# Weighting and turning the gathered expert rows by products with diagonal matrices on the tensor engine

## The chip, the cores and the metric

One Trainium2 chip, one core. The metric is the device time of one execution of the whole program in microseconds (us), median of several runs. TensorE is called PE below, VectorE DVE, ScalarE ACT, GpSimd POOL, SyncE SP. "PEclk" or "granted clock" is TensorE's clock as a share of 2.4 GHz: 1.00 is 2.4 GHz and 0.50 is 1.2 GHz.

## What is computed

Two layers of a hybrid backbone over 256 latent and 256 context tokens of width 1024. Each layer first mixes tokens (attention, a long convolution, a short convolution) and then runs a mixture of 16 experts, of which two work for each token. The end of a layer is the part that matters here: for each token the rows of its two experts are weighted, added, multiplied by a per-channel gate and added to x. The next layer starts with a root-mean-square norm of that x and a modulation by shift and scale.

```python
wts = jnp.take_along_axis(s, eidx, axis=1)
wts = wts / jnp.sum(wts, axis=-1, keepdims=True)
...
y = (jax.nn.silu(t @ w_gate[e]) * (t @ w_up[e])) @ w_down[e]
out = out + combine[:, e:e + 1] * y
...
x = x + gt2 * y[:, :s]
xc = xc + cgt2 * y[:, s:]
...
y = xf * lax.rsqrt(jnp.mean(xf * xf, axis=-1, keepdims=True) + NORM_EPS)
```

## The kernel before

The program is written engine by engine: each engine has its own list of instructions, run in the order of the code, and semaphores tie them together. Nothing reorders them. x lives in SBUF as `xT`, channels on partitions (8 tiles `k` of 128) and 512 tokens along the free axis. The experts' outputs are written as token rows to a tensor in DRAM, `y_rows`.

The passage of this case lies between the two layers (`l` = 0 at its end, called the passage below). It is walked once, for four groups `t` of 128 tokens:

- ACT issues the last four DMAs of expert outputs into `y_rows` (line 1240). DVE waits until all of them have landed (lines 2136 and 2137, semaphore `y_out`) and sets `rows_ok`.
- POOL waits for `rows_ok`, then issues eight indirect DMAs (line 833), two for each `t`, which gather the rows of the token's first and second expert into `yg[:, t, 0, :]` and `yg[:, t, 1, :]`, 512 KB each.
- ACT scales the first row by its weight into `comb` (`scale_first`, lines 1344 to 1349), DVE multiplies the second by its weight and adds it (line 2148), PE turns the sum with eight transposes (line 2846, shown in the trace under the helper's line 2181), and DVE multiplies the result by the gate and adds it to `xT` in eight steps (line 2156).
- For the next layer's norm ACT squares the new `xT` (`next_square`, lines 1351 to 1355), PE sums the squares over channels with a matrix of ones (`next_sums`, line 2833, eight products for each `t`), DVE scales the sums (line 2165), ACT takes the root (line 1375) and DVE the reciprocal (line 2168). The two halves of the tokens (latent, context) have one root each. Then DVE clears the semaphores (line 2171), and that sets `layer_done`, for which all engines wait.

Beside it the next layer's weights are prepared. SP issues eight loads of 1 MB of modulation weights, the leads 0 to 7 (in the trace `lead<-in_mod`, and `spare<-in_mod` for leads 6 and 7), then two loads of 1 MB of input weights (`stage<-in_in`, `unit(l + 1, ...)`), and a third of modulation weights (`stage<-in_mod`) once PE has used lead 6 (lines 738 to 750). PE multiplies the leads by the conditioning vector (`lead_units`, line 2223 in the trace) after its last expert work; leads 4 to 7 share one wait, for all four. The two input weights are split into a high part by ACT (`whi`, line 1361) and a rest by DVE (`wlo`, lines 2141 to 2143, in the trace under line 1391). `modulation` (line 1439) is a group of three small DVE steps on the result of the leads.

## Time and profile before

| what | value |
|---|---|
| median of 3 runs | 1332.89 us (1331.44 to 1336.42) |
| profiled execution | 1330.76 us |
| its span | 1328.9 us |
| mean granted clock of TensorE | 0.959 |
| PE busy | 1215.8 us, 91% |
| DVE busy | 661.7 us, 50% |
| ACT busy | 412.9 us, 31% |
| POOL busy | 128.4 us, 10% |
| passage, from the landing of the last expert rows to the clearing of semaphores | 777.6 to 812.0 us |

The span is the time between the first and the last recorded instruction; the profiled execution's own time is 1.9 us longer. The shares are averages over the whole program; what is changed lies in one stretch of 34 us, and that stretch has to be read by itself, in the chain of waits and in the engines' timelines. In a timeline row a group of like instructions is merged: start, time to the end of the last, engine, line, what, count, and in brackets the idle time before them and what ended it.

### The profile page before, as it was taken

Reading aid. Unit: us, or ns where it says so; the run is one execution under the profiler, and the core shown is the slowest. Engines: PE = TensorE matmul, PEld = TensorE weight load, DVE = VectorE, ACT = ScalarE, POOL = GpSimd, SP = SyncE. Lnnn points to the kernel's source line nnn. Section 1 sums busy time; section 2 is a strip of 40 time slices with the busy share of each in tenths; the row PEclk is TensorE's granted clock in tenths of the full one; section 3 lists DMA queues with packets and bytes.
Section 4 is the critical chain, followed back from the end, with each engine's and each line's share of the span. In section 5 each row is a group of like instructions: output and inputs, shape, how many; then the busy total and the mean of one; then the engine's idle time right before and its main releaser. Section 6 shows DMA issues by size and latency. Waiting matters only on the chain.

```text
span 1328.9 us, 20293 instructions
## 1 busy us (share of the span) xinstructions
PE 1215.8 (91%) x8260; PEld 841.7 (63%) x8260; DVE 661.7 (50%) x1166; ACT 412.9 (31%) x662; POOL 128.4 (10%) x121
## 2 busy tenths in 40 slices
PE   3799999999999989999999947999999989998996
PEld 1577678787887733778774336787799835443443
DVE  2727468687547272535331336477876562221222
ACT  2523324443244220334331036435555420000000
POOL 0000000000005021000000030008930210000000
PEclk9799999999999989999999878999999989998998
DMA  9734459474435559999999973885244789999997
GB/s 376 303 145 190 190 206 377 162 214 182 190 153 195 199 207 422 399 390 406 402 409 393 417 284 116 336 329 202 96 159 165 302 312 387 402 389 401 396 421 290
DMA packets 58576, 382.47 MB, mean 288 GB/s; under 512 B 8464, under 2 KB 10836, under 8 KB 18996
## 3 DMA queue, kind: packets, MB, share of 16 engines
q1 hardware_dynamic: 45584, 345.00, 66.3%
q0 software_dynamic: 4688, 18.50, 3.8%
q10 hardware_dynamic: 8212, 17.69, 3.7%
q8 instruction: 65, 1.06, 0.3%
q14 instruction: 27, 0.22, 0.0%
HBM read 363.58 MB, written 44.84 MB: 307 GB/s over the span
## 4 chain that ended last, share of the span: by engine, by line
PE 25%; issue 20%; DMA 10%; DVE 5%; ACT 3%; POOL 2%; DVEq 0%; SPq 0%; POOLq 0%; ACTq 0%
DMA wexp<-in_expert 7%; PE bank L2696 5%; PE bank L2711 3%; PE bank L2213 3%; PE bank L2214 3%; PE bank L2215 3%; DMA x_rows<-trow,rowid 2%; PE bank L2729 1%; PE bank L2181 1%; PE bank L2223 1%; POOL m_lo L795 1%; DVE wlo L1391 1%; DMA stage<-in_in 1%; PE bank L2305 1%; DVE xT L1397 1%
## 5 line engine op out<-in xcount | busy, mean ns | idle before, releaser
L2213 PE MATMUL bank<-h_hi,whi 128*128 128x512 f32 (+1 forms) x640 | 223.9, 350 | 15.1 <-DVE h_lo L1391 10.7
L2214 PE MATMUL bank<-h_lo,whi 128*128 128x512 f32 (+1 forms) x640 | 219.0, 342 | 0.0
L2215 PE MATMUL bank<-h_hi,wlo 128*128 128x512 f32 (+1 forms) x640 | 218.8, 342 | 0.0
L2696 PE MATMUL bank<-wexp,xg 128*32 128x512 f32 (+1 forms) x1104 | 183.9, 603 | 6.6 <-DMA wexp<-in_expert 3.7
L1391 DVE TENSOR_TENSOR wlo<-stage,whi 128x2048 fp32r<-128x2048 f32 x56 | 133.2, 2386 | 40.7 <-ACT whi L843 27.7
L2213 PEld LDWEIGHTS bank<-h_hi,whi 128*128 128x128 f32 x640 | 123.3, 193 | 38.9 <-issue 13.4
L2215 PEld LDWEIGHTS bank<-h_hi,wlo 128*128 128x128 f32 x640 | 123.1, 192 | 13.7
L2214 PEld LDWEIGHTS bank<-h_lo,whi 128*128 128x128 f32 x640 | 123.2, 192 | 13.4 <-issue 0.5
L843 ACT ACTIVATE whi<-stage 128x2048 fp32r<-128x2048 f32 x56 | 107.0, 1910 | 57.4 <-PE bank L2215 39.4
L2696 PEld LDWEIGHTS bank<-wexp,xg 128*32 128x32 f32 (+1 forms) x1104 | 53.1, 123 | 110.9 <-issue 100.6
L2711 PE MATMUL bank<-wexp,act_a 128*32 128x256 f32 (+1 forms) x864 | 103.7, 473 | 10.6 <-DMA wexp<-in_expert 8.1
L1391 DVE TENSOR_TENSOR act_a<-act_s,bank 128x128 f32<-128x128 f32 (+1 forms) x35 | 12.2, 349 | 195.4 <-ACT act_s L843 195.4
L2711 PEld LDWEIGHTS bank<-wexp,act_a 128*32 128x32 f32 (+1 forms) x864 | 37.1, 123 | 58.9 <-issue 39.3
L843 ACT ACTIVATE yrow<-bank 128x512 f32<-128x512 f32 (+1 forms) x28 | 13.7, 490 | 178.4 <-PE bank L2711 109.8
L2047 DVE COPY gu_sb<-bank 128x512 f32<-128x512 f32 x35 | 24.1, 690 | 88.7 <-PE bank L2696 88.7
L1391 DVE TENSOR_TENSOR wexp_lo<-wexp,hring 128x1024 fp32r<-128x1024 f32 x36 | 42.2, 1222 | 31.0 <-ACT hring L843 30.7
L1397 DVE SCALAR_TENSOR_TENSOR conv<-glu,vec,conv 128x512 f32<-128x512 f32 (+1 forms) x90 | 57.0, 675 | 0.9 <-DVE amp L1391 0.3
L2603 PE MATMUL bank<-x_hi,wexp_lo 128*128 128x256 f32 x192 | 55.1, 287 | 0.0
L2602 PE MATMUL bank<-x_lo,hring 128*128 128x256 f32 x192 | 54.3, 283 | 0.0
L2601 PE MATMUL bank<-x_hi,hring 128*128 128x256 f32 x192 | 53.9, 281 | 0.0
L2213 PE MATMUL bank<-m_hi,whi 128*128 128x512 f32 (+1 forms) x128 | 45.0, 351 | 4.3 <-POOL m_lo L795 4.2
L780 POOL TENSOR_SCALAR tap<-glu,vec 128x256 f32<-128x256 f32 x30 | 45.2, 1508 | 2.9
(371 smaller groups left out, 1986.3 us busy)
## 6 DMA issues: line engine op xcount, KB each, us to landing
wexp<-in_expert SPq DMA_DIRECT2D x190, 1024.0 KB, 15.4
stage<-in_in SPq DMA_DIRECT2D x40, 1024.0 KB, 8.4
raw<-in_mod SPq DMA_DIRECT2D x18, 1024.0 KB, 6.5
stage<-in_mod SPq DMA_DIRECT2D x16, 1024.0 KB, 4.9
x_rows<-in_c_zero SPq DMA_DIRECT2D x32, 512.0 KB, 8.5
y_rows<-in_c_zero SPq DMA_DIRECT2D x20, 512.0 KB, 8.5
spare<-in_mod SPq DMA_DIRECT2D x8, 1024.0 KB, 17.1
stage<-in_out SPq DMA_DIRECT2D x8, 1024.0 KB, 4.8
```

The source lines that it names most:

```text
L780: p.then(nc.gpsimd.tensor_scalar(tap[:, :], src, w, None, MUL))
L843: return nc.scalar.activation(out_, in_, f, **kw)
L1391: return V.tensor_tensor(o, x, y, op)
L1397: return V.scalar_tensor_tensor(out=o, in0=x, scalar=s, in1=y, op0=op0, op1=op1)
L2213: MM(o, w[0], x_[0], start=start, stop=False)
L2214: MM(o, w[0], x_[1], start=False, stop=False)
L2215: return MM(o, w[1], x_[0], start=False, stop=stop)
L2601: MM(o, hi_, x_hi[:, i, :], start=False, stop=False)
L2602: MM(o, hi_, x_lo[:, i, :], start=False, stop=False)
L2603: ins = MM(o, lo_, x_hi[:, i, :], start=False, stop=(i == KT - 1 and f == 1))
L2696: ins = MM(bank[0][g * w:(g + 1) * w, :], x_[:, 2 * j + k, :], weights[:, c], start=(first_ == 0), stop=(last_ == 0))
L2711: ins = MM(bank[3][h * w:(h + 1) * w, 0:8 * w], a_[:, kk, :], wexp[:, z, 4 + j, c], start=(kk == 0), stop=(kk == 3))
```

## The change

Groups of edits, all at the end of layer 0:

1. `comb` is gone, and with it ACT's `scale_first` and DVE's weighted addition. DVE makes `comb_w` once, eight diagonal 128x128 matrices (two experts, four token groups) with the tokens' weights on the diagonal. PE multiplies `yg` (128 tokens by 128 channels, the stationary operand) by the diagonal matrix: that weights and turns it at once, and the second product adds the second expert's row into the same bank. Sixteen products take the place of eight transposes for each `t`.
2. DVE's two rests (`wlo`) stand ahead of its wait for `y_out` and of `rows_ok`, where they stood behind it. `modulation` and the scaling of the first half's sums stand ahead of the last group's additions to `xT`.
3. SP issues the two input weights ahead of leads 6 and 7.
4. ACT loads the table of the root ahead of the passage; the root of the first half stands ahead of the last group's square. DVE's reciprocal of the first half stands ahead of the scaling of the second half's sums.

```diff
-        comb = at_byte("comb", [P, 2, D], f32, R3)
+        comb_w = at_byte("comb_w", [P, 2, 4, P], f32, R3)
...
+                    for i in range(RING - 1):
+                        sp.wait_ge(S(f"used0{i}"), plan.uses[0])
+                        unit(l + 1, orders[l + 1].issue[i])
                     for i, j in ((RING - 1, LEAD - 2), (EC - 1, LEAD - 1)):
                         sp.wait_ge(S(f"used0{i}"), plan.uses[0])
                         lead_load(j)
-                    for i in range(RING - 1):
-                        sp.wait_ge(S(f"used0{i}"), plan.uses[0])
-                        unit(l + 1, orders[l + 1].issue[i])
...
-                def scale_first(t):
-
-                    act.wait_ge(sem("all", f"yg{t}"), (l + 1) * 2 * 16 + (16 if t < XR - 1 else 32))
-                    if t >= 2:
-                        act.wait_ge(S("combT"), t - 1)
-                    fn(comb[:, t % 2, :], yg[:, t, 0, :], ACT.Copy, scale=tokv[:, 1, t:t + 1]).then_inc(S("scaled"), 1)
...
+                    nc.scalar.preload_act_table(ACT.Sqrt)
                     for t in range(NT):
-                        scale_first(t)
...
-                    for t in range(NT - 2, NT):
-                        next_square(t)
                     for half in range(2):
                         c = slice(half * SEQ, (half + 1) * SEQ)
+                        next_square(NT - 2 + half)
...
+                    shape = [P, 2, NT, P]
+                    eye = ident[:, :].unsqueeze(1).unsqueeze(1).to_broadcast(shape)
+                    tt(comb_w[:, :, :, :], eye, tokv[:, 1:3, 0:NT].unsqueeze(3).to_broadcast(shape), MUL).then_inc(S("scaled"), 1)
+                    for p in range(2):
+                        dve.wait_ge(S("hi"), len(parts) + p + 1)
+                        rest(l + 1, p).then_inc(S("lo"), 1)
                     dve.wait_ge(S("y_heavy"), 64 * len(plan.heavies) + CONV_TILES)
                     dve.wait_ge(S("y_out"), (count + STEPS - len(plan.heavies)) * 64)
                     dve.sem_inc(S("rows_ok"), 1)
-                if l < DEPTH - 1:
-
-                    for p in range(2):
-                        dve.wait_ge(S("hi"), len(parts) + p + 1)
-                        rest(l + 1, p).then_inc(S("lo"), 1)
...
                 for t in range(NT + 1 if l < DEPTH - 1 else 0):
-                    if t < NT:
-
-                        dve.wait_ge(S("scaled"), t + 1)
-                        stt(comb[:, t % 2, :], yg[:, t, 1, :], tokv[:, 2, t:t + 1], comb[:, t % 2, :], MUL, ADD).then_inc(S("combined"), 1)
+                    if t == NT:
+
+                        modulation(0, order.batches + 1, l + 1, LEAD_BANK)
+                        next_mean(0)
...
-                    pe.wait_ge(S("combined"), t + 1)
+                    pe.wait_ge(S("scaled"), 1)
+                    pe.wait_ge(sem("all", f"yg{t}"), (l + 1) * 2 * 16 + (16 if t < XR - 1 else 32))
                     if t >= 2:
                         pe.wait_ge(S("x_moe"), (t - 1) * KT)
                     for k in range(KT):
                         b = 2 * (t % 2) + k // 4
-                        ins = T_(bank[b][:, (k % 4) * P:(k % 4 + 1) * P], comb[:, t % 2, k * P:(k + 1) * P])
+                        for c in range(2):
+                            ins = MM(bank[b][:, (k % 4) * P:(k % 4 + 1) * P], yg[:, t, c, k * P:(k + 1) * P], comb_w[:, c, t, :], start=(c == 0), stop=(c == 1))
```

How the rows stand on SP at the end of layer 0, before (`lead_133` and `lead_134` are leads 4 and 5, `spare_115` and `spare_118` leads 6 and 7, `stage_49` and `stage_50` the two input weights, `stage_51` the third load):

```order
L712 DMA lead_133<-in_mod 128x2048 [waits H_ok]
L712 DMA lead_134<-in_mod 128x2048
L712 DMA spare_115<-in_mod 128x2048 [waits used02]
L712 DMA spare_118<-in_mod 128x2048 [waits used05]
L657 DMA stage_49<-in_in 128x2048 [waits used00]
L657 DMA stage_50<-in_in 128x2048 [waits used01]
L657 DMA stage_51<-in_mod 128x2048 [waits mod]
```

and in the changed kernel:

```order
L712 DMA lead_133<-in_mod 128x2048 [waits H_ok]
L712 DMA lead_134<-in_mod 128x2048
L657 DMA stage_49<-in_in 128x2048 [waits used00]
L657 DMA stage_50<-in_in 128x2048 [waits used01]
L712 DMA spare_115<-in_mod 128x2048 [waits used02]
L712 DMA spare_118<-in_mod 128x2048 [waits used05]
L657 DMA stage_51<-in_mod 128x2048 [waits mod]
```

The two input weights have moved ahead of leads 6 and 7.

On DVE in the passage, before (the row "ISA" is the increment of `rows_ok` with its waits; the wait for `y_out` is printed on the next row; `rs` holds the sums and then the roots):

```order
L2137 ISA [waits cf_n]
L1391 TENSOR_TENSOR wlo_55<-stage_49,whi_52 128x2048 [waits y_out,hi]
L1391 TENSOR_TENSOR wlo_56<-stage_50,whi_53 128x2048 [waits hi]
L1397 SCALAR_TENSOR_TENSOR comb<-yg,tokv,comb 128x1024 [waits scaled] x2
L1397 SCALAR_TENSOR_TENSOR xT<-bank,modT,xT 128x128 [waits combT]
L1397 SCALAR_TENSOR_TENSOR xT<-bank,modT,xT 128x128 x7
L1397 SCALAR_TENSOR_TENSOR comb<-yg,tokv,comb 128x1024 [waits scaled]
```

and in the changed kernel:

```order
L1383 TENSOR_TENSOR comb_w<-tables,tokv 128x1024
L1383 TENSOR_TENSOR wlo_55<-stage_49,whi_52 128x2048 [waits hi]
L1383 TENSOR_TENSOR wlo_56<-stage_50,whi_53 128x2048 [waits hi]
L2135 ISA [waits cf_n]
L1389 SCALAR_TENSOR_TENSOR xT<-bank,modT,xT 128x128 [waits y_out,combT]
L1389 SCALAR_TENSOR_TENSOR xT<-bank,modT,xT 128x128 x7
```

The two rests now stand ahead of `rows_ok`, and the weighted additions are gone.

On PE, token groups 1 and 2, before:

```order
L2181 MATMUL bank<-tables,comb 128x128 [waits combined]
L2181 MATMUL bank<-tables,comb 128x128 x7
L2833 MATMUL bank<-sq_n,tables 128x128 [waits sq_ok]
L2833 MATMUL bank<-sq_n,tables 128x128 x7
L2181 MATMUL bank<-tables,comb 128x128 [waits x_moe,combined]
L2181 MATMUL bank<-tables,comb 128x128 x7
```

and in the changed kernel:

```order
L2842 MATMUL bank<-comb_w,yg 128x128 [waits yg1_all,scaled]
L2842 MATMUL bank<-comb_w,yg 128x128 x15
L2827 MATMUL bank<-sq_n,tables 128x128 [waits sq_ok]
L2827 MATMUL bank<-sq_n,tables 128x128 x7
L2842 MATMUL bank<-comb_w,yg 128x128 [waits x_moe,yg2_all,scaled]
L2842 MATMUL bank<-comb_w,yg 128x128 x15
```

The place in the queue is the same; the wait is for the gather itself, and there are sixteen products instead of eight transposes.

## Rows read from the trace of the kernel before

**Rows 1.** Chain of waits through the passage: start us, us, engine and line.

```profile
784.51 5.75 DMA yg<-y_rows,rowid
...
806.69 1.28 ACT L843
...
808.43 1.76 DVE rs L2168
810.22 0.43 DVE rs L1394
810.68 0.49 ACT rs L843
811.16 0.82 DVEq L2171
```

**Rows 2.** Instructions that touch `comb`: count, duration in ns, first and last start.

```profile
L843 ACT ACTIVATE comb<-yg,tokv x4: 1133/1148/1149, 787.2 to 795.8; 128x1024 f32<-128x1024 f32 x4
L1397 DVE SCALAR_TENSOR_TENSOR comb<-yg,tokv,comb x4: 1277/1281/1285, 788.4 to 798.0; 128x1024 f32<-128x1024 f32 x4
L2181 PE MATMUL bank<-tables,comb x32: 272/364/476, 789.7 to 803.1; 128*128 128x128 f32 x32
```

**Rows 3.** Instructions of line 2833, the 32 products of `next_sums`.

```profile
L2833 PE MATMUL bank<-sq_n,tables x64: 274/275/582, 796.0 to 808.5; 128*128 128x128 f32 x64
```

**Rows 4.** Timeline of PE around the passage.

```profile
768.02 1.91 PE L2223 MATMUL bank<-lead,cst 128*32 128x256 f32 x32
...
789.73 1.97 PE L2181 MATMUL bank<-tables,comb 128*128 128x128 f32 x8 [14.04 <-DVE comb L1397]
...
795.96 3.49 PE L2833 MATMUL bank<-sq_n,tables 128*128 128x128 f32 x16 [1.19 <-ACT sq_n L843]
799.28 1.04 PE L2181 MATMUL bank<-tables,comb 128*128 128x128 f32 x8
800.16 1.95 PE L2833 MATMUL bank<-sq_n,tables 128*128 128x128 f32 x16
801.94 0.52 PE L2232 MATMUL bank<-tables,modrow 128*128 128x16 f32 x4
```

**Rows 5.** Timeline of SP: issues of leads 6 and 7 and of the input weights.

```profile
747.22 10.08 SPq L712 DMA_DIRECT2D spare<-in_mod  x2
757.35 0.91 SPq L657 DMA_DIRECT2D stage<-in_in  x2
```

**Rows 6.** Tile `spare` (leads 6, 7) from 690 us: issue to landing.

```profile
L712 SPq DMA_DIRECT2D spare<-in_mod x2: 327/380/432, 747.2 to 757.0; - x2
...
DMA to landing us min/median/max: 15.0/18.4/21.8
```

**Rows 7.** Tile `stage`, 740 to 800 us: the split of the two input weights, and landing.

```profile
L657 SPq DMA_DIRECT2D stage<-in_in x2: 430/430/431, 757.3 to 757.8; - x2
L843 ACT ACTIVATE whi<-stage x2: 1910/1910/1910, 774.7 to 777.4; 128x2048 fp32r<-128x2048 f32 x2
L1391 DVE TENSOR_TENSOR wlo<-stage,whi x2: 2286/2289/2292, 777.6 to 779.8; 128x2048 fp32r<-128x2048 f32 x2
L657 SPq DMA_DIRECT2D stage<-in_mod x1: 328/328/328, 774.9 to 774.9; - x1
...
DMA to landing us min/median/max: 5.6/17.3/19.5
```

**Rows 8.** Timeline of ACT: the last four issues of expert rows.

```profile
769.88 1.81 ACTq L1240 DMA_DIRECT2D y_rows<-yrow  x4
```

**Rows 9.** Timeline of DVE: the wait for the last expert rows, and group 0's additions.

```profile
777.61 4.50 DVE L1391 TENSOR_TENSOR wlo<-stage,whi 128x2048 fp32r<-128x2048 f32 x2 [11.39 <-DMA y_rows<-yrow]
...
792.66 2.15 DVE L1397 SCALAR_TENSOR_TENSOR xT<-bank,modT,xT 128x128 f32<-128x128 f32 x8
```

**Rows 10.** Timeline of POOL: one scatter of layer 0, and the first three gathers.

```profile
489.24 1.03 POOL L811 DMA_INDIRECT x_rows<-trow,rowid  x1 [71.25 <-DVE rowid L1947]
...
777.80 2.98 POOL L833 DMA_INDIRECT yg<-y_rows,rowid  x1 [249.64 <-DVEq L2138]
781.09 1.87 POOL L833 DMA_INDIRECT yg<-y_rows,rowid  x1 [0.30 <-issue]
783.26 0.94 POOL L833 DMA_INDIRECT yg<-y_rows,rowid  x1 [0.30 <-issue]
```

**Rows 11.** Windows: busy us of PE, PEld, DVE, ACT, POOL; granted clock, DMA share, GB/s.

```profile
778.00:780.00 2.00, 0.00 (x0) 0.00 (x0) 2.00 (x2) 1.30 (x1) 2.00 (x1) 0.63 0.52 217
...
798.00:800.00 2.00, 2.00 (x16) 2.00 (x15) 1.27 (x2) 1.06 (x1) 0.00 (x0) 0.75 0.00 0
```

More of the change, by code:

```diff
@@ L2138, in _, with next_mean @@
                     dve.sem_inc(S("rows_ok"), 1)
-                if l < DEPTH - 1:
-                    for p in range(2):
-                        dve.wait_ge(S("hi"), len(parts) + p + 1)
-                        rest(l + 1, p).then_inc(S("lo"), 1)
+                def next_mean(half):
+                    c = slice(half * SEQ, (half + 1) * SEQ)
+                    dve.wait_ge(S("sq_sum"), 2 * KT + 1 + 2 * (half + 1))
+                    ts(rs[:, c], bank[5 + half][:, c], 1.0 / D, EPS, MUL, ADD).then_inc(S("mean_sq"), 1)
                 for t in range(NT + 1 if l < DEPTH - 1 else 0):
-                    if t < NT:
-                        dve.wait_ge(S("scaled"), t + 1)
-                        stt(comb[:, t % 2, :], yg[:, t, 1, :], tokv[:, 2, t:t + 1], comb[:, t % 2, :], MUL, ADD).then_inc(S("combined"), 1)
+                    if t == NT:
+                        modulation(0, order.batches + 1, l + 1, LEAD_BANK)
+                        next_mean(0)
                     if t >= 1:
@@ L2158, in _ @@
                 if l < DEPTH - 1:
-                    modulation(0, order.batches + 1, l + 1, LEAD_BANK)
-                    for half in range(2):
-                        c = slice(half * SEQ, (half + 1) * SEQ)
-                        dve.wait_ge(S("sq_sum"), 2 * KT + 1 + 2 * (half + 1))
-                        ts(rs[:, c], bank[5 + half][:, c], 1.0 / D, EPS, MUL, ADD).then_inc(S("mean_sq"), 1)
-                        if half == 0:
-                            dve.wait_ge(S("root"), 6)
-                            v.then(V.reciprocal(rs[:, c], rs[:, c]))
+                    dve.wait_ge(S("root"), 6)
+                    v.then(V.reciprocal(rs[:, 0:SEQ], rs[:, 0:SEQ]))
+                    next_mean(1)
                     dve.wait_ge(S("root"), 7)
```

## The prediction, made before the changed kernel was run

> **What bounds the kernel now.** The page gives PE 91% of the span, but the change touches only the passage between the layers, so the share says nothing here. I read the chain of waits through that stretch first. It runs from the landing of the last expert rows over POOL, the gather, ACT, DVE and PE to the clearing of the semaphores at 811.16 us, 0.82 us long [rows 1]. All engines wait for it, so whatever the passage gains or loses goes one for one into the end. Then I read each engine's timeline for what stands ahead of each link. DVE is released at 777.61 by the last expert rows, and POOL's first gather starts at 777.80 [rows 9, 10]. The first token group is there at 787.2, when ACT starts its scaling [rows 2]; PE gets it at 789.73 [rows 4]. The semaphores are cleared by 811.98. The reader should see three things: two gathers take 2.98 and 1.87 us where the third takes 0.94 [rows 10]; PE runs at half clock until about 799 us [rows 11]; and a table load of 1.28 us and a reciprocal of 1.76 us stand one behind the other at the very end [rows 1].
>
> **Part 1, when the gather may start.** SP's new order gives the two input weights the places of leads 6 and 7. These were issued at 747.2 and 757.0 and landed 21.8 and 15.0 us later, at 769.0 and 772.0 [rows 6]; the input weights came behind them, at 774.7 and 777.3 (757.35 plus 17.3, 757.8 plus 19.5) [rows 5, 7]. Landings followed the order of issue, 2.6 to 3 us apart, so the DMA engines were full, and I take the same four landing times with the loads exchanged: input weights at 769 and 772, leads 6 and 7 at 774.7 and 777.3. ACT can't split before its last issue of expert rows, which ends at 769.88 + 1.81 = 771.7 [rows 8]. Two high parts of 1.91 us end at 773.6 and 775.5; two rests of 2.29 us on DVE end at 776.0 and 778.3 [rows 7]. The expert rows land at 777.6 as before, since the same bytes compete. Before, `rows_ok` waited for them alone; now the last rest ends later: the gather is let go at 778.3, **0.7 us later**. `comb_w` (one DVE step over 128x1024; the nearest row is the 1.28 us of `comb` [rows 2]) lies in the 11.4 us in which DVE idled before 777.6 [rows 9] and costs nothing; the whole of that idle time would have to be used up before it did.
>
> **Part 2, the gathers.** Before, both rests ran on DVE from 777.6 to 782.1, beside the first two gathers. The first gather ends at 780.78, that is 0.9 us after the first rest (779.9); the second at 782.96, 0.9 us after the second (782.1); 0.94 us is what an undisturbed gather takes, and an indirect DMA after a pause of 71 us took 1.03 [rows 9, 10]. So each gather waited for a rest to end. With the rests done first both take 0.94, which saves 2.04 + 0.93 = 2.97 us. The first starts at 778.4, the second at 779.65 (0.94 and the gap of 0.30). A pair has landed 5.75 us after its second gather began [rows 1], so at 785.4 instead of 787.2.
>
> The page "SBUF — State Buffer" of the Trainium skill, in its part on which operations take the pair of ports shared by DVE and GpSimd, says that a tensor_tensor takes only the read side, and infers that writing descriptors isn't held up by it; it also says that a GpSimd operation that reads SBUF is. By the first sentence nothing would be saved here, and the time would be that of the second rival below. The rows agree with the second sentence: these gathers read their row numbers from SBUF.
>
> Against this stands the third load, `stage<-in_mod`. It waits for PE's use of lead 6, and PE begins leads 4 to 7 only when all have landed, 777.3 instead of 772.0. It was issued at 774.9 and done 5.6 us later [rows 7], before the gather's data moved. Two units of leads take 1.75 us at full clock (1.91 with the tail) [rows 4] and twice that at half; after 5.6 us without work PE will be at half clock (it fell within 778 to 780, about 3 us after its last product [rows 11]). The third unit ends at about 782, and 1 MB then flows into the gathers of groups 0 and 1. It costs group 0 between nothing (group 0 is in front) and 2.6 us (the whole megabyte first, at the spacing above). I take 0.8, as only the last 2 us of group 0 can overlap. **PE starts at 786.3.**
>
> **Part 3, PE.** Eight products of line 2833 leave 16 records (64 records for 32 products [rows 3]); eight transposes leave eight (32 for 32 [rows 2]). At full clock 16 records take 801.94 - 800.16 = 1.78 us and eight transposes 800.16 - 799.28 = 0.88 [rows 4], 0.111 us a record either way. The new products have the same shape and type as those of line 2833, so a group of sixteen is 32 records, 3.56 us at full clock, four times the transposes; at half clock, by eight records in 1.97 [rows 4], close to 7. PE now sets the pace: its 3.56 + 1.78 us a group is more than the 3 us between gathers, and DVE's additions (2.15 [rows 9]) with ACT's square (1.06) take 3.3 beside it. At full clock: four groups 14.2, sums of groups 0 and 1 3.6, the small products 0.4 [rows 4], then after the last group its additions, square and sums, 0.1 + 2.15 + 1.1 + 1.95 = 5.3 (the sums of group 2 lie under them). Total 23.5: **786.3 + 23.5 = 809.8**. What is taken off ACT and DVE (1.15 and 1.28 us, four times [rows 2]) is off the path with it; only its first link, 2.5 us from 787.2 to 789.7, was on it.
>
> **Part 4, the tail.** The table load goes under the wait for the gather, the reciprocal of the first half under the last group's work, and modulation and the first root too; what hides them is 5 us of PE and ACT work. Left are the scaling of the second half, its root and the clearing, 810.22 to 811.98 = 1.76 us before [rows 1]. From 809.8 with 0.1 of hand-over: **811.6, against 811.98: 0.4 us sooner**. What follows in layer 1 starts from `layer_done` and is moved as a whole. The profiled execution's 1330.76 becomes 1330.4; the same 0.4 off the median 1332.89 gives **1332.5**.
>
> **The rivals.**
> - *PE starts group 0 at half clock.* By the above the leads end at 782.5 to 784, so PE idles 2 to 4 us before group 0, and about 3 us sufficed for a fall [rows 11]. It came back 3 us after the steady work that began at 795.96 [rows 4, 11]. 3 to 5 us at half clock lose 1.5 to 2.5: 0.4 sooner becomes 1.6 later, 1334.5.
> - *The gathers are slow for another reason* (first use after 250 us), as the first sentence of the page above would have it: 2.97 us stay, and the third load then collides less (0.8 back). 1332.5 + 2.2 = 1334.7. Against it: both ends fit the ends of the rests.
> - *The input weights don't land earlier*, so that the reorder doesn't do what it says. Every microsecond of the second landing past 773.6 holds `rows_ok` by one. At the old 777.3 the rest ends at 781.5, 3.2 later: 1335.7.
> - *Slower for good: the passage stays at half clock.* Then the four groups and the three exposed sums, 128 + 48 records, cost 0.11 more each: 19.4 us, 1352. It decides from about 60 records at half clock on (6.7 us, 0.5%). Against it: the clock rose under sums and transposes at 799 [rows 11], and PE has less idle time now.
>
> **How the numbers follow.** A measurement of this kernel can tell about 0.5% (6.7 us) from no change. Chances: forecast 0.42, half clock at group 0 0.24, slow gathers 0.12, late weights 0.12, half clock for good 0.05, something not seen 0.05, spread to both sides. All but the last two lie within 0.5%. The bounds of the third load's cost (nothing to 2.6) put the forecast at 1331.7 to 1334.3; the rivals reach 1335.7, two of them together 1339; the runs before spread from 1.5 below to 3.5 above their median. The range is 1327 to 1339. Faster 0.05, within 0.5% 0.87, slower 0.08.
>
> **What would show it.** Right: gathers of 0.94 us each, the first starting at 778 to 779; both rests over before it; the third load issued at about 782; 128 records of the new products, 32 in 3.6 us from the second group on; no table load behind the last square; clearing near 811. Wrong: a first gather of 2 us or more with DVE idle; a `hi` that waits for its load behind 772; granted clock of 0.5 after 790; ACT reloading a table at a square; or a moved start of layer 1 that isn't found again at the end.

## The result, and the profile after

The changed kernel takes 1338.43 us (median of 16 runs, 1328.59 to 1343.78) against 1334.24 of the kernel before beside it: ratio 1.003, 95% interval [1.0016, 1.0044]. It is slower by about 4 us. The prediction had said 0.4 us sooner, in a range of 1327 to 1339 us: the time lies inside the range, but it moved the other way, and clear of the noise. The profiled execution took 1336.22 us with a span of 1334.4, 5.5 more than before.

TensorE's timeline of the changed kernel through the passage (start, time to the end of the last, what, and in brackets the idle time before and what ended it):

```profile
777.80 3.60 PE L2217 MATMUL bank<-lead,cst 128*32 128x256 f32 x32 [3.78 <-DMA spare<-in_mod]
781.21 1.91 PE L2217 MATMUL bank<-spare,cst 128*32 128x256 f32 x32
785.95 3.81 PE L2842 MATMUL bank<-comb_w,yg 128*128 128x128 f32 x32 [2.83 <-DMA yg<-y_rows,rowid]
791.68 3.81 PE L2842 MATMUL bank<-comb_w,yg 128*128 128x128 f32 x32 [1.93 <-DMA yg<-y_rows,rowid]
...
802.84 3.82 PE L2842 MATMUL bank<-comb_w,yg 128*128 128x128 f32 x32
```

Group 0 starts at 785.95 where its transposes started at 789.73 [rows 4]; each group takes 3.7 to 3.8 us to the end of its last product, and group 1 waits 1.93 us for its gather. The chain of waits names that gather and shows the tail:

```profile
783.04 8.51 DMA yg<-y_rows,rowid
...
810.00 2.07 PE bank L2827 x16
...
812.16 0.44 DVE rs L1386
812.60 0.02 issue
812.62 0.48 ACT rs L843
813.11 0.82 DVEq L2165
```

8.51 us from its second gather to landing, where the one on before's chain took 5.75 [rows 1]. The semaphores are cleared at 813.93, 1.95 later than before. POOL's timeline with the first two gathers:

```profile
778.68 1.53 POOL L833 DMA_INDIRECT yg<-y_rows,rowid  x1 [249.80 <-DVEq L2136]
780.52 0.98 POOL L833 DMA_INDIRECT yg<-y_rows,rowid  x1 [0.30 <-issue]
```

DVE's timeline with the rests:

```profile
774.84 4.49 DVE L1383 TENSOR_TENSOR wlo<-stage,whi 128x2048 fp32r<-128x2048 f32 x2 [7.38 <-ACT whi L843]
```

SP's timeline with the third load:

```profile
782.33 0.33 SPq L657 DMA_DIRECT2D stage<-in_mod  x1
```

I cut every profiled execution at the same marks. The passage goes from the end of ACT's last issue of expert rows (771.69 before [rows 8], 772.64 after) to the first `hn` step of layer 1 (812.3 before, 814.25 after). Layer 1 goes from there to the end of the span, and its attention part ends where POOL's last eight `m_lo` begin. "Place" is by how many records TensorE's list ahead of layer 1 is longer than before's.

| kernel | place | passage | layer 1 | its attention part | time (median) | ratio to before |
|---|---|---|---|---|---|---|
| before | 0 | 40.6 | 516.6 | 216.8 | 1332.89 | |
| e8 before again | 0 | 41.6 | 517.8 | 217.7 | 1335.57 (one run) | |
| e3 transposes kept | 0 | 40.2 | 518.2 | 217.6 | 1334.22 | 1.0006 [0.9994, 1.0019] |
| e7 the same, third load held | 0 | 38.3 | 517.6 | 217.8 | 1330.66 | 0.9981 [0.9965, 0.9997] |
| e12 e7 again | 0 | 37.5 | 517.8 | 217.6 | 1328.95 | 0.9959 [0.9945, 0.9973] |
| after | 96 | 41.6 | 520.2 | 219.4 | 1338.43 | 1.0030 [1.0016, 1.0044] |
| e1 after again | 96 | 44.1 | 521.1 | 218.4 | 1340.12 | 1.0054 [1.0034, 1.0073] |
| e2 before, products | 96 | 43.7 | 523.4 | 220.3 | 1340.21 | 1.0049 [1.0033, 1.0064] |
| e4 after, third load held | 96 | 41.0 | 521.8 | 218.5 | 1336.68 | 1.0021 [1.0007, 1.0035] |
| e14 after, old order of loads | 96 | 45.0 | 520.7 | 219.9 | 1339.83 | 1.0034 [1.0017, 1.0051] |
| e6 before, idle products | 96 | 40.8 | 520.9 | 220.0 | 1335.96 | 1.0011 [0.9996, 1.0027] |
| e11 e7, increments | 96 | 51.8 | 523.5 | 219.8 | 1349.06 | 1.0093 [1.0070, 1.0115] |
| e9 after, idle products | 128 | 43.4 | 519.0 | 217.8 | 1334.80 | 1.0009 [0.9991, 1.0027] |
| e10 e4, idle products | 128 | 42.6 | 516.7 | 216.9 | 1334.42 | 0.9993 [0.9978, 1.0008] |
| e13 e4, idle products behind | 128 | 39.5 | 520.8 | 217.8 | 1333.28 | 0.9993 [0.9976, 1.0011] |
| e5 three products | 160 | 52.4 | 517.7 | 217.0 | 1341.10 | 1.0055 [1.0036, 1.0074] |

Each ratio is taken against the kernel before run beside it on the same chip, where its median was 1333.5 to 1334.8 us, so ratios can be compared between rows and medians less well; a ratio is estimated from the single runs and differs from the quotient of the medians by up to 0.0014. A passage is one profiled execution: it repeated to 1.0 us in the kernel before (40.6, 41.6) and to 2.5 in the changed kernel (41.6, 44.1), and layer 1 to 1.2 and 0.9.

The 5.5 us of the two profiled spans are therefore 0.9 of layer 0, which the change doesn't touch and whose end scatters between 770.5 and 775.3 in all sixteen; 1.0 of the passage; and 3.6 of layer 1. The 1.0 of the passage alone is no more than it repeats to; the 3.6 of layer 1 is. Two questions follow: why the passage didn't get shorter, and why layer 1 got longer.

### The profile page after: what moved, and what is told of

It is laid out like the page before. It is cut to its first block, busy times and chain, and to the rows that moved or that the text cites. A ratio compares the mean times of both kernels' runs of the same rounds, so it can differ in the third digit from the quotient of the medians.

```text
span 1334.4 us, 20477 instructions
## 1 busy us (share of the span) xinstructions
PE 1226.8 (92%) x8356; PEld 851.7 (64%) x8356; DVE 658.6 (49%) x1163; ACT 408.4 (31%) x658; POOL 122.9 (9%) x121
## 4 chain that ended last, share of the span: by engine, by line
PE 25%; issue 20%; DMA 12%; DVE 5%; ACT 2%; POOL 2%; SPq 0%; DVEq 0%; POOLq 0%; ACTq 0%
DMA wexp<-in_expert 8%; PE bank L2690 4%; PE bank L2207 3%; PE bank L2705 3%; PE bank L2208 3%; PE bank L2209 3%; DMA x_rows<-trow,rowid 2%; PE bank L2175 1%; PE bank L2723 1%; PE bank L2842 1%; PE bank L2217 1%; POOL m_lo L795 1%; DMA yg<-y_rows,rowid 1%; PE bank L2487 1%; PE bank L2299 1%
## 5 line engine op out<-in xcount | busy, mean ns | idle before, releaser
L2705 PE MATMUL bank<-wexp,act_a 128*32 128x256 f32 (+1 forms) x864 | 105.3, 482 | 13.3 <-DMA wexp<-in_expert 8.9
L1389 DVE SCALAR_TENSOR_TENSOR xT<-bank,modT,xT 128x256 f32<-128x256 f32 (+1 forms) x64 | 22.7, 410 | 61.2 <-PE bank L2209 38.0
```

Source lines behind the costliest of these rows:

```text
L1389: return V.scalar_tensor_tensor(out=o, in0=x, scalar=s, in1=y, op0=op0, op1=op1)
L2705: ins = MM(bank[3][h * w:(h + 1) * w, 0:8 * w], a_[:, kk, :], wexp[:, z, 4 + j, c], start=(kk == 0), stop=(kk == 3))
```

## Experiments on the passage

**e1, the changed kernel again**, for the base on the chip of e2 to e4. No edit.

> The changed kernel once more, unchanged, for a second profile. The passage is taken from the end of the last issue of expert rows to the first step of layer 1 on DVE: 40.6 us in the profile of before (771.7 to 812.3), 41.6 in that of after (772.6 to 814.25). Theory A, the loss is in the passage (products on the pace, the third load in the gather of group 1): 41.6 again within 0.5, and what follows in layer 1 is as long as before, 516.6 us, give or take what it varies by. Theory B, the loss is in layer 1 (520.2 us in the profile of after, against 516.6, with the clock at half from 914 to 921 us): again 519 to 521. Time 3 to 5 us over the kernel before by either.

The passage took 44.1 us, not 41.6 within 0.5, and layer 1 was long again (521.1). TensorE's timeline:

```profile
793.88 5.37 PE L2842 MATMUL bank<-comb_w,yg 128*128 128x128 f32 x32 [2.75 <-DMA yg<-y_rows,rowid]
```

The windows there (busy us of PE, PEld, DVE, ACT, POOL; granted clock; DMA share, GB/s):

```profile
792.00:794.00 2.00, 0.12 (x1) 0.16 (x1) 1.32 (x6) 0.65 (x1) 0.00 (x0) 0.93 1.03 418
794.00:796.00 2.00, 2.00 (x10) 2.00 (x11) 0.00 (x0) 0.41 (x1) 0.00 (x0) 0.50 0.97 395
```

Here group 1 waited 2.75 us instead of 1.93, the clock fell to 0.50 behind that wait, and the group took 5.37 us instead of 3.81. The DMA engines were full, at 400 GB/s: the third load had gone out at 784.10.

**e2, the kernel before with the products alone.**

```diff
-                        ins = T_(bank[b][:, (k % 4) * P:(k % 4 + 1) * P], comb[:, t % 2, k * P:(k + 1) * P])
+                        for c in range(2):
+                            ins = MM(... yg[:, t, c, k * P:(k + 1) * P], comb_w[:, c, t, :], start=(c == 0), stop=(c == 1))
```

> The kernel before with the products in place of scaling, adding and transposing, and nothing else moved: rests still behind the release of the gather, loads in the old order, table load and reciprocal at the end. Theory A: group 0 is there at the old time, PE starts 2.5 us sooner than before but takes 3.6 instead of 0.9 us a group; the passage becomes 40.6 - 2.5 + 4 (longer chain of PE work, 24 instead of 19 us from its start) = 42 to 43 us, at half clock at its start up to 45; the time is 2 to 5 us over before. Theory B (layer 1): the passage 42 to 43 and layer 1 3 to 4 us longer as well.

**e3, the changed kernel with its moves, and `comb` and the transposes kept**: the same lines the other way.

> The changed kernel with scaling, adding and transposing as before: all moves kept (loads, rests, table load, root, modulation), only the products undone. Theory A: the moves alone gain, 1.8 us by the earlier gather and 3 by table load and reciprocal off the end, less 1 to 2 for the third load in the gather: passage 36.5 to 38.5 us, time 2 to 4 us under before. Theory B: the passage is as short, but layer 1 is 3 to 4 us longer and the time is that of before, within 2 us.

TensorE's timeline in e2:

```profile
789.50 9.37 PE L2839 MATMUL bank<-comb_w,yg 128*128 128x128 f32 x64 [10.47 <-DMA yg<-y_rows,rowid]
```

In e3, ACT's wait for group 0's rows:

```profile
789.46 1.15 ACT L843 ACTIVATE comb<-yg,tokv 128x1024 f32<-128x1024 f32 x1 [11.09 <-DMA yg<-y_rows,rowid]
```

And TensorE's timeline there:

```profile
791.98 1.97 PE L2184 MATMUL bank<-tables,comb 128*128 128x128 f32 x8 [8.87 <-DVE comb L1397]
794.71 1.97 PE L2184 MATMUL bank<-tables,comb 128*128 128x128 f32 x8 [0.77 <-DVE comb L1397]
```

The products alone make the passage 2 to 3 us longer (43.7 against 40.6 and 41.6): behind 10.47 us without work TensorE begins at half clock and takes 9.37 us for two groups that would take 7.4. The moves alone bring nothing that can be measured, 40.2 where 36.5 to 38.5 was expected. Groups 0 and 1 of the transposes are at half clock too, and it costs them little, because a transposed group leaves TensorE waiting: e8, the kernel before at half clock for 23.9 us instead of 20.5, had a passage 1.0 us longer.

Which group the third load hits is decided by tenths of a microsecond. In e3 it left 1.34 us after the second gather of group 0 had begun, in e5 1.65 and in e9 0.04 after, and group 0's rows then landed 8.46, 8.20 and 7.70 us behind that gather. In the changed kernel it left 1.81 and in e1 2.32 after, group 0 landed in 5.29 and 5.39, and group 1 took 8.51 and 9.43.

**e4, the changed kernel with the third load held until the last gather has landed.**

```diff
                     sp.wait_ge(S("mod"), order.batches * BATCH + LEAD - 1)
+                    sp.wait_ge(sem("all", "yg3"), (l + 1) * 2 * 16 + 32)
                     unit(l + 1, orders[l + 1].issue[RING - 1])
```

> The changed kernel with one wait more on SP: the third load (modulation weights of layer 1) is issued only when the last gather has landed, so nothing competes with the gathers. Theory A with the collision as a cause: group 1 lands 5.8 us after its second gather was issued instead of 8.6, PE has no gap of 1.9 us between groups 0 and 1, passage 39.5 to 40 us, 1.9 us under the changed kernel. If PE alone sets the pace: the gap goes and the passage is the same within 0.5. Either way the third load lands by about 800 and is wanted at 824.

TensorE's timeline:

```profile
785.67 9.01 PE L2843 MATMUL bank<-comb_w,yg 128*128 128x128 f32 x64 [3.62 <-DMA yg<-y_rows,rowid]
```

The wait of group 1 is gone: 64 records in one piece. But the first of them ran at half clock, so the passage fell only to 41.0 instead of below 40.

**e7, the kernel of e3 with the same hold**, and **e12, e7 once more.**

> All moves kept, the products undone, and the third load held until the last gather has landed. Theory A: without the collision the gathers land 3 us apart, the passage is 38 to 39.5 us instead of 40.2 and the time 1 to 2 us under before, faster than both kernels. If the passage of the transposing kernel is paced by something other than the gather (ACT and DVE), 40.2 stays.

> The kernel with all moves, transposes kept and the third load held, once more, as the partner of the kernel with 192 increments on the same chip and to see whether it beats the kernel before again. Expected 1330 to 1331.5, ratio 0.997 to 0.9985, passage 38 to 39, layer 1 517 to 518. By both theories it is the same; if layer 1 scatters by 3 us here, both theories on layer 1 lose their base.

Passage 38.3 and 37.5, time 1330.66 and 1328.95. This version beats both kernels: ratio 0.9981 [0.9965, 0.9997], and again 0.9959 [0.9945, 0.9973], a little better than expected. By the passages the third load therefore cost the kernel with transposes 1.9 to 2.7 us, and held it costs nothing that shows in layer 1 (517.6 and 517.8).

**e5, three products where the change has two** (the first expert's product is issued twice; the second one starts the sum anew, so the first is overwritten and the values stay).

```diff
-                        for c in range(2):
-                            ins = MM(... yg[:, t, c, k * P:(k + 1) * P], comb_w[:, c, t, :], start=(c == 0), stop=(c == 1))
+                        for i, c in enumerate((0, 0, 1)):
+                            ins = MM(... yg[:, t, c, k * P:(k + 1) * P], comb_w[:, c, t, :], start=(i < 2), stop=(i != 1))
```

> The changed kernel with the first expert's product issued twice (the first one is overwritten), so 24 products, 48 records, for each group instead of 16 and 32; the values are the same. Theory A (PE sets the pace of the passage): each group takes 16 records more at 0.111 us, 1.78 us, four times 7.1; the first gap behind group 0 swallows up to 2 of it, so the passage is 5 to 7 us longer than the changed kernel's 41.6 to 44.1, and the time 5 to 7 us over it, some 1344 to 1346. Theory C (PE's work is hidden, the gather or DVE sets the pace): under 2 us more. If layer 1 (520 to 523 us with the products, 516.6 and 518.2 without) gets longer by more PE instructions ahead of it, it is longer here again, 523 and more.

TensorE's timeline:

```profile
786.67 13.90 PE L2842 MATMUL bank<-comb_w,yg 128*128 128x128 f32 x96 [5.88 <-DMA yg<-y_rows,rowid]
```

The passage grew by 8 to 11 us, more than the 5 to 7 expected. Four groups of 16 more records at full clock are 7.1 us: TensorE sets the pace, as the prediction had it. The rest has two sources in this trace: group 0's rows came late, behind the third load, and TensorE, idle for 5.88 us, began it at half clock (8.54 us for its 48 records, 5.5 to 5.6 in the later groups).

**e13, e4 with 16 idle products behind the leads**, ahead of group 0. It asks whether the clock, or the gathers' landing, makes up what the products still cost. e10 (below) has the same 16 ahead of the leads.

```diff
                     lead_units()
+                    for i in range(16):
+                        MM(bank[7][:, 0:P], ones[:, :], ident[:, :], start=True, stop=True)
```

> The changed kernel with the third load held, and the 16 idle products now behind leads 4 to 7 (ahead of group 0) where they stood ahead of them. With them ahead, TensorE then idled 4.36 us, the granted clock was 0.50 from 786 to 792, groups 0 and 1 took 10.06 us together and the passage 42.6 us; transposes and a held third load take 37.5 to 38.3. Theory 'clock': what the products still cost is that they set the pace while the clock is at half. The idle products fill the 4.4 us, group 0 starts at full clock, groups 0 and 1 take 7.2 to 7.5 us, the passage 39.5 to 40.5; the list is 128 records longer again, so layer 1 stays at 516.7 to 518 and the time is 1331.5 to 1333. Rival 'landing': groups 0 and 1 are paced by the gathers' landing and not by the clock; they stay at 9 to 10 us with gaps in them, the passage at 42 and the time at 1334 to 1335.

TensorE's timeline in e10:

```profile
786.71 10.06 PE L2846 MATMUL bank<-comb_w,yg 128*128 128x128 f32 x64 [4.36 <-DMA yg<-y_rows,rowid]
```

In e13:

```profile
782.02 3.84 PE L2834 MATMUL bank<-tables 128*128 128x128 f32 x32
786.24 7.38 PE L2845 MATMUL bank<-comb_w,yg 128*128 128x128 f32 x64 [0.38 <-DMA yg<-y_rows,rowid]
```

7.38 us for the same 64 records, a passage of 39.5 against 42.6. The gathers land in time; it was the clock: 2.7 of the 3.1 us lie in these 64 records. The times don't show it, the ratio is 0.9993 in both, and e13's layer 1 was 4.1 us longer than e10's in the profiles (see below). At full clock and without the collision the products are still 1.2 to 2 us behind the transposes of e7 and e12.

**e14, the changed kernel with SP's loads in the old order** (leads 6 and 7 first). It undoes that edit alone.

```diff
+                    for i, j in ((RING - 1, LEAD - 2), (EC - 1, LEAD - 1)):
+                        sp.wait_ge(S(f"used0{i}"), plan.uses[0])
+                        lead_load(j)
                     for i in range(RING - 1):
                         sp.wait_ge(S(f"used0{i}"), plan.uses[0])
                         unit(l + 1, orders[l + 1].issue[i])
```

> The changed kernel with SP's loads in the order of before: leads 6 and 7 ahead of the two input weights, all else as changed. Leads 4 to 7 are then done at about 773 to 775 and the third load is issued at 775 to 776, ahead of all gathers; the input weights land at 774.7 and 777.3, the rests end at 781 to 782 and the gather is let go with the last of them. Prediction's rival 'late weights': gather released 3 us later, passage about 3 us longer than the changed kernel's 41.6 to 44.1. Theory 'the third load is what the new order costs': the 2 to 3 us that the third load took from the gathers come back, the two cancel, passage 41 to 44 and the time 1336 to 1339. Layer 1 stays long (519 to 523), since TensorE's list is 96 records longer.

POOL's timeline, the first gather:

```profile
780.15 2.76 POOL L833 DMA_INDIRECT yg<-y_rows,rowid  x1 [253.56 <-DVEq L2136]
```

DVE's timeline, the rests:

```profile
777.03 2.29 DVE L1383 TENSOR_TENSOR wlo<-stage,whi 128x2048 fp32r<-128x2048 f32 x1 [9.65 <-ACT whi L843]
779.74 2.29 DVE L1383 TENSOR_TENSOR wlo<-stage,whi 128x2048 fp32r<-128x2048 f32 x1 [0.42 <-ACT whi L843]
```

The second rest ended at 782.03 and the first gather at 782.91. The third load had left at 776.02, ahead of the gathers, and group 0 started at 788.82 behind 12 us of idleness, at half clock (9.89 us for 64 records). Passage 45.0, the longest of those with two products a channel block and above the 41 to 44 expected: by the passages the new order of the loads was worth 1 to 3 us to the products, although it also makes the third load collide. The times don't tell the two orders apart (1.0034 against 1.0030 and 1.0054).

## Experiments on layer 1

After e1 to e5 layer 1 stood out: 520.2 to 523.4 in after, e1, e2 and e4, 516.6 to 518.2 in before and e3, and 517.7 in e5. The long ones have in common that TensorE's list is 96 records longer. The first place where they part is 80 to 105 us into layer 1. DMA queue 8 of the profile's third section carries instructions; it moves one block of 16 KB at a time, 65 in before and 66 in after, and between two of them TensorE runs 127 products on average. So 96 records more shift the borders of the blocks by 96, 128 shift them by nearly nothing, and 160 by about 32. (The Trainium skill, page "Advanced Engine Details and Errata", section "ISA Cache", gives a line of 16 KB as 256 instructions; a product with its weight load is two, and 127 products a block agree with that.)

**e6, the kernel before with 48 idle products (96 records) in TensorE's idle time ahead of the passage.**

```diff
                     lead_units()
+                    for i in range(48):
+                        MM(bank[7][:, 0:P], ones[:, :], ident[:, :], start=True, stop=True)
```

> The kernel before with 48 products of the new shape (96 records, as many more than the changed kernel has) issued on PE behind the leads, into a bank that nothing reads, in the 14 us in which PE has nothing to do before group 0. It adds the instructions and the work and no time on the path: they end at about 787 and group 0 is there at 789.7. Theory A: time and layer 1 as before, within 1.5 us, perhaps 1 us less since PE is at full clock when group 0 comes. Theory B (the longer list of PE instructions or the warmer engine makes layer 1 longer): layer 1 at 520 to 523 us and the time 3 us over before.

**e8, the kernel before again**, with a profile.

> The kernel before once more, for a second profile: passage 40.6 us within 0.5, since its transposes wait for ACT and DVE and hardly depend on the clock; layer 1 is 516.6 in the first profile. If layer 1 varies by itself, it comes out anywhere between 516 and 522; if the products make it longer, it is 516 to 518 here.

e6's passage is that of before (40.8), and layer 1 is long (520.9); e8's is short (517.8), though its passage was 41.6 and not 40.6 within 0.5. So layer 1's loss isn't due to the products' results, nor to the passage's length. The time of e6 alone isn't told from before: 1.0011 [0.9996, 1.0027], where the 3.1 to 4.3 us that its layer 1 has over the two profiles of before would be 1.0023 to 1.0032. Its times show the loss less clearly than its profile.

**e9, the changed kernel with 16 idle products ahead of leads 4 to 7**, which makes 128.

```diff
+                        if j == EARLY_LEADS:
+                            for i in range(16):
+                                MM(bank[7][:, 0:P], ones[:, :], ident[:, :], start=True, stop=True)
                         if j in (0, EARLY_LEADS):
```

> The changed kernel with 16 idle products (32 records, 128x128, result never used) put on TensorE's list ahead of its wait for leads 4 to 7, where it idles 3.8 us (774.0 to 777.8). They fit into that gap at full clock (16 x 0.22 = 3.6 us), so the passage stays 41.6 us, or 41 if the clock gains. Theory 'place on the list': layer 1 is 3 to 5 us longer wherever TensorE's list is 96 records longer ahead of it, and not where it is 0 or 160 longer, because TensorE's instructions come by DMA in blocks of 16 KB and a block holds about 127 records. With 96 + 32 = 128 records the blocks' borders stand where they stood before: layer 1 comes back from 520.2 to between 516.6 and 518, and the time falls by about 3.5 us, 1338.4 to 1335. Rival 'more work ahead' (more products in the passage make the clock fall later in layer 1): 128 records are more than 96, layer 1 stays 520 to 523 and the time 1338 to 1340.

**e10, e4 with the same edit.**

> The changed kernel with its third load held until the last gather has landed, and with the same 16 idle products ahead of leads 4 to 7. It puts both corrections together. Held third load alone gave 1336.7 with a passage of 41.0 and a layer 1 of 521.8. Theory 'place on the list': layer 1 falls to 516.6 to 518, time 1332 to 1333.5. Rival 'more work ahead': layer 1 stays at 520 to 523, 1336 to 1338. The passage says beside it whether products cost anything once the load is out of the way: 38.3 us is what the transposes took so; the products at full clock should take 39.5 to 40, at half clock in their first groups 41 to 42.

**e11, e7 with 192 increments of a semaphore nobody waits for**, 96 at either of the two places: as many instructions as 96 records have, and no product.

```diff
+                            for i in range(96):
+                                pe.sem_inc(sem("all", "passed"), 1)
```

> The kernel with all moves, transposes kept and the third load held (1330.66, passage 38.3, layer 1 517.6), with 192 increments of a semaphore nobody waits for on TensorE's list: 96 ahead of its wait for leads 4 to 7 and 96 behind the leads, both in idle time. 192 instructions are what 96 records are (a weight load and a product each), but no product is computed. Theory 'place on the list': layer 1 is 520 to 522, the time 1334 to 1335. Rival 'more work ahead': no work was added, layer 1 stays 517 to 518 and the time 1330.7. If the increments take longer than the gaps (over 50 ns each) the passage grows; it is read apart.

Layer 1 as a whole came back in e10 (516.7) and only in part in e9 (519.0, expected under 518). The attention part took 217.8 and 216.9 us in e9 and e10, and 219.8 in e11, whose only difference from e12 (217.6) is instructions that compute nothing. "More work ahead" falls; the place on the list decides. Over all sixteen profiles the attention part is 216.8 to 217.8 us in the nine with a place of 0, 128 or 160, and 218.4 to 220.3 in the seven with 96. e11's increments took 0.14 us each, not under 0.05, and made its passage 14 us longer; that is why its time says nothing. e9's passage didn't stay at 41.6 either: with the leads done sooner the third load left at 781.1 and held up group 0, which started at 788.86.

**What happens at that place.** The DMA queues of the changed kernel from 893.5 to 894.5 (packets, MB, share of 16 engines):

```profile
q8 instruction: 1, 0.02, 7.0%
```

SP's timeline there:

```profile
893.25 0.33 SPq L657 DMA_DIRECT2D stage<-in_mod  x1
894.11 1.03 SPq L657 DMA_DIRECT2D raw<-in_mod  x1
895.24 0.38 SPq L657 DMA_DIRECT2D stage<-in_in  x1
```

The same three issues in e10:

```profile
894.57 0.33 SPq L657 DMA_DIRECT2D stage<-in_mod  x1
895.43 0.33 SPq L657 DMA_DIRECT2D raw<-in_mod  x1
895.86 0.38 SPq L657 DMA_DIRECT2D stage<-in_in  x1
```

In all seven kernels with a place of 96 the block of instructions comes 79.4 to 79.6 us behind the first `hn`, and the issue of `raw`, at 79.8, takes 0.96 to 1.39 us. In the nine others the block comes at 74.6 to 76.2, and the issue takes 0.33. The load behind it comes later by as much. ACT's timeline in e12, where it splits that load (88.7 us behind `hn`):

```profile
898.49 1.91 ACT L844 ACTIVATE whi<-stage 128x2048 fp32r<-128x2048 f32 x1 [2.63 <-DMA stage<-in_in]
```

And in e11 (89.7 behind `hn`):

```profile
915.62 1.91 ACT L844 ACTIVATE whi<-stage 128x2048 fp32r<-128x2048 f32 x1 [3.62 <-DMA stage<-in_in]
```

DVE's rest follows it, and behind the rest on DVE stand the steps for which TensorE's next transposes wait. TensorE's timeline in before:

```profile
912.72 1.09 PE L2181 MATMUL bank<-tables,probs 128*128 128x128 f32 x8 [2.05 <-DVE probs L1394]
```

In after:

```profile
915.42 1.97 PE L2175 MATMUL bank<-tables,probs 128*128 128x128 f32 x8 [2.74 <-DVE probs L1386]
```

That wait is 1.99 to 2.19 us in the nine kernels and 2.74 to 4.67 in the seven: so every kernel with a place of 96 loses 0.6 to 2.6 us there. The clock falls beside it. The windows of before (columns as above):

```profile
916.00:918.00 2.00, 2.00 (x19) 2.00 (x19) 1.93 (x5) 0.86 (x3) 1.82 (x3) 1.00 0.64 180
```

And of after:

```profile
916.00:918.00 2.00, 2.00 (x9) 1.49 (x9) 2.00 (x1) 1.18 (x3) 1.90 (x2) 0.50 0.00 0
```

It falls to 0.50 in all seven, and for 3.4 us also in five of the nine (e3, e7, e9, e12, e13). Those five have an attention part of 217.6 to 217.8 us and the other four 216.8 to 217.7, so a fall of that length costs at most 1 us. In e1, e4 and e14 it lasted 3.4 us as well; in after, e2, e6 and e11 it lasted 6.8. An estimate: taking what the wait has over 2.05 off what the attention part has over 216.8 leaves about 0.5 us in the first three and 1.7 to 2.0 in the other four, so that in the changed kernel the half clock cost more (about 1.9) than the longer wait (0.7). It is rough, since e8's attention part, with neither, is 0.9 longer than that of before.

That the block holds the issue, and doesn't only come beside it, is read from the ends of both. Over all sixteen profiles 27 issues of `raw` began more than 0.25 us into a block of queue 8. In 26 of those 27 the issue ended 0.33 to 0.38 us behind the end of the block, one ordinary issue later, though the blocks took 0.88 to 1.33 us and the issues 0.37 to 1.39; the other took 0.33. The eight that began just before a block or less than 0.25 us into one took 0.33; away from a block an issue took at most 0.52, apart from one of over 2.1 in each kernel. Where the held issue falls matters: in e5, where layer 1 isn't longer, it was an earlier one, 58.8 us behind `hn`:

```profile
881.71 1.22 SPq L657 DMA_DIRECT2D raw<-in_mod  x1
```

What is not settled: the 17 issues of `stage<-in_mod` that fell into a block all took 0.33, and no run shows why `raw` is held and they aren't. And the attention part is not all: of after's 3.6 us in layer 1 it holds 2.6, and the experts' part some more. From POOL's scatter of layer 1 to the end it is 242.8 to 244.5 us in eleven of the sixteen, and 246.1 to 248.1 in e1, e2, e4, e11 and e13, which have places of 96 and 128. In e13 TensorE waited 2.28 us for its last expert weights (1.40 in before), and the clock fell to 0.50 behind that. This part is where e13's layer 1 became 520.8 and not under 518 as I expected, so a place of 128 doesn't bring back all of layer 1. I didn't find what makes that load late.

## Why the prediction was wrong, step by step

- **Part 1, release of the gather: the number right, by luck.** 778.3 was forecast, POOL started at 778.68. The new order worked: ACT split both input weights in one piece from 772.90. But the release wasn't set by the last rest, as the sum had it. The last expert rows landed at 778.36, 5.7 us behind ACT's last issue as in the kernel before (5.8), DVE set `rows_ok` at 778.38, and the last rest ended at 779.33. Layer 0 had ended 0.9 later, which happened to be about what the rest was to cost. DVE's increment didn't wait for the rest in front of it to finish; in e14 it went at 779.85, just behind the start of the last rest (779.74) and 2.2 before its end.
- **Part 2, slow gathers: right in kind.** Every gather that began beside a rest ended 0.9 us behind the rest: 782.91 and 782.03 in e14, 780.21 and 779.33 in after, whose first took 1.53 us instead of the 0.94 forecast, since the last rest still ran. Every other gather of the sixteen profiles that took more than 0.99 us ran beside DVE's addition into `comb` and ended 0.8 us behind that; the rest took 0.94 to 0.98. The rival "slow for another reason" falls. (The Trainium skill, page "SBUF — State Buffer", section "Who interferes with whom", has a DVE step with two SBUF inputs contend with GpSimd's reads, and these rows agree. It also infers that a tensor_tensor doesn't hold up the writing of descriptors; these indirect DMAs were held up, and no run here shows whether at the reading of their row numbers or at the descriptors.)
- **Part 2, the third load: the step that failed in the passage.** I had it leave at 782 (782.33), flow into the gathers of groups 0 and 1, and cost group 0 0.8 us and group 1 nothing. Group 0 had its rows 5.4 us behind the second gather and paid nothing. Group 1 paid: 8.51 us to landing, 1.93 us of idle TensorE, 2.75 in e1. e7 against e3 prices the collision at 1.9 us, e4 against after and e1 at 0.6 to 3.1, with half clock in e4's group 0 in it.
- **Part 3: right but for that wait and its consequence.** A group takes 3.6 to 3.8 us, and TensorE sets the pace (e5). From group 0's start to the last sum took 26.1 us, not 23.5: 1.9 are the wait, and most of the other 0.7 is that the four groups took 14.9 and not 14.2. What I had as a rival, half clock at group 0, was the case in e2, e4, e5, e9, e10 and e14; in the two profiled executions of the change it wasn't. e13 against e10 prices it at up to 3.1 us, where the prediction had 1.5 to 2.5. The forecast took the clock to be full in the likeliest case, and a pace set by TensorE makes each microsecond of half clock count, where with transposes it hardly did.
- **Part 4, the tail: right.** From the last sum (812.07) to the clearing (813.93) are 1.86 us; 1.76 and 0.1 were forecast.
- **"What follows in layer 1 is moved as a whole": the step that failed by most.** Layer 1 was 3.6 us longer. The prediction named such a thing only as a sign of being wrong and gave it no price. 96 more records on TensorE's list moved the blocks of its instructions, one of them onto an issue of SP; the attention part, where that shows, holds 2.6 of the 3.6 us; the rest stays open.
- By the sum: the passage was to end 0.4 sooner; it came 1.0 later in the profiled execution (0.9 of layer 0 apart), and layer 1, which had no term, added 3.6. That the time still lies inside the range is luck: the range was spread for the passage's rivals and the scatter of the runs, and most of the loss came from neither. Its upper end, "two of them together 1339", is also a little high by its own prices: late weights and slow gathers together make 1337.9.

## What to carry to other kernels

Moving work from idle engines to the one that then sets the pace makes every gap and every half-clock stretch in front of it count, so the sum should be made at half clock too, where that engine idles ahead. A load that a new order lets go at another time should be followed to each transfer behind it, not to the first alone: here one wait on SP (e7 against e3, ratio 0.9981 against 1.0006) was worth more than all the moves together. And when a part that wasn't touched changes its length, look at where the instruction blocks of a long list now fall, and shift them by padding before judging the edit.

## What the runs showed of the hardware that I hadn't expected

- TensorE's instructions come in blocks of 16 KB, one for about 127 products, and an issue of `raw` on SP that began more than 0.25 us into a block ended 0.33 to 0.38 us behind the block's end, 26 times of 27; issues of `stage<-in_mod` weren't held. Padding by 32 records brought the changed kernel's ratio from 1.0030 [1.0016, 1.0044] to 1.0009 [0.9991, 1.0027], and e4's from 1.0021 [1.0007, 1.0035] to 0.9993 [0.9978, 1.0008]. The intervals overlap in the first pair and just touch in the second, and the padding also changed the passage; the profiles, not the times, show where the gain lies.
- A semaphore increment on DVE passed ahead of the end of the step before it: `rows_ok` went out at 778.38, the rest ended at 779.33 (779.85 and 782.03 in e14).
- 96 increments on TensorE's list took 13.3 us, 0.14 each (e11).
- A load of 1 MB issued 0.04 to 1.65 us after the second gather of group 0 had begun made that group's rows land 7.7 to 8.5 us behind it instead of 5.2 to 6.0; issued 1.81 or 2.32 us after, it left group 0 alone and made group 1 land in 8.5 and 9.4.
- TensorE idled 2.83 us ahead of group 0 in after and began at a clock of 1.00; behind 2.75 us in e1 it began at 0.50. The length of a wait alone didn't decide it.
